# Gathering the rows of six heads for the first four tokens while the other two heads are picked

## The reference

```python
def block(xblk):
    q = (xblk @ w_q).astype(jnp.float32).reshape(PEER_BLOCK, PEER_HEADS, 2, PEER_DK // 2)
    s1 = jnp.einsum('thd,kd->thk', q[:, :, 0], k1)
    s2 = jnp.einsum('thd,kd->thk', q[:, :, 1], k2)
    t1, i1 = lax.top_k(s1, PEER_TOPK)
    t2, i2 = lax.top_k(s2, PEER_TOPK)
    ...
    top, pos = lax.top_k(cand, PEER_TOPK)
    eidx = jnp.take_along_axis(cidx, pos, axis=-1)
    gate = jax.nn.softmax(top, axis=-1).astype(xblk.dtype)
    u = expert_u[eidx]
    act = jax.nn.gelu(jnp.einsum('td,thkd->thk', xblk, u))
    v = expert_v[eidx]
    return jnp.einsum('thk,thkd->td', gate * act, v)
```

## Time and profile before

| | |
|---|---|
| median of 3 runs | 3699.09 us (3698.78 to 3702.22) |
| the profiled execution | 3699.25 us, its span 3697.4 us |
| PE busy | 3109.4 us (84%) |
| PE weight load busy | 2080.7 us (56%) |
| DVE busy | 1774.6 us (48%) |
| ACT busy | 613.5 us (17%) |
| POOL busy | 788.1 us (21%) |
| moved by DMA | 1096 MB, of which 671 MB by POOL's gathers |
| chain that ended last | PE 44%, DMA 28%, DVE 16%, issue 8% |

### The profile page before, as it was taken

How to read it: one execution, slowest core, us unless ns; L and a number is a source line. 1 busy time by engine, 2 the same in 40 slices (tenths; PEclk the granted TensorE clock), 3 DMA queues, 4 the chain that set the end, 5 groups by cost and what they waited for, 6 DMA issues and landing times.

```text
span 3697.4 us, 49910 instructions
## 1 busy us (share of the span) xinstructions
PE 3109.4 (84%) x17550; PEld 2080.7 (56%) x17550; DVE 1774.6 (48%) x4188; ACT 613.5 (17%) x1631; POOL 788.1 (21%) x891
## 2 busy tenths in 40 slices
PE   8998999999998999999999999888655666665564
PEld 7766777777776699998888887555300000000000
DVE  2397656665665200017333333468944444444444
ACT  1001222222222100001111111121211111111211
POOL 1000111211121000001222222233333333333332
PEclk9999999999999999999999999888755555555555
DMA  5434333333332688877999999999999999999997
GB/s 196 144 124 142 120 120 121 122 119 120 121 126 82 229 285 294 293 243 286 420 418 419 417 419 417 412 408 417 365 416 418 418 418 415 418 417 415 413 417 295
DMA packets 203478, 1096.05 MB, mean 296 GB/s; under 512 B 27360, under 2 KB 69216, under 8 KB 75952
## 3 DMA queue, kind: packets, MB, share of 16 engines
q0 software_dynamic: 92160, 671.13, 44.2%
q1 hardware_dynamic: 104096, 401.31, 30.2%
q10 hardware_dynamic: 7120, 22.22, 1.5%
HBM read 1062.88 MB, written 31.70 MB: 296 GB/s over the span
## 4 chain that ended last, share of the span: by engine, by line
PE 44%; DMA 28%; DVE 16%; issue 8%; POOL 2%; ACT 2%; DVEq 0%; SPq 0%; ACTq 0%; POOLq 0%
PE psum L519 27%; DMA branches<-in_peer_u,idx 22%; PE psum L605 7%; DMA ring<-in_peer_u,idx 4%; DVE branches L1431 2%; PE psum L974 2%; DVE branches L1929 2%; DVE branches L1534 2%; PE psum L684 1%; PE psum L675 1%; DVE ring L1929 1%; PE psum L681 1%; DVE rs L1642 1%; POOL ring L2017 1%; PE psum L349 1%
## 5 line engine op out<-in xcount | busy, mean ns | idle before, releaser
L1929 DVE CUSTOM_DVE_ANT_0 ring<-ring,psum 128x1024 f32<-128x1024 f32 x480 | 566.7, 1218 | 624.5 <-DMA ring<-in_peer_u,idx 575.7
L519 PE MATMUL psum<-hT,ring 128*128 128x128 f32 (+2 forms) x4800 | 801.6, 328 | 19.3 <-DMA ring<-in_w_glu 9.0
L519 PEld LDWEIGHTS psum<-hT,ring 128*128 128x128 f32 x4800 | 718.4, 195 | 94.5 <-issue 22.4
L957 PE MATMUL psum<-shared,selb 24*128 24x512 bf16 x1280 | 300.9, 520 | 451.8 <-DVE dots L1929 448.7
L957 PEld LDWEIGHTS psum<-shared,selb 24*128 24x128 bf16 x1280 | 56.1, 96 | 1017.1 <-DVE dots L1929 926.2
L605 PE MATMUL psum<-hT,ring 128*128 128x320 f32 x2112 | 621.6, 436 | 1.0 <-issue 1.0
L605 PEld LDWEIGHTS psum<-hT,ring 128*128 128x128 f32 x2112 | 381.8, 191 | 142.0 <-issue 18.4
L1291 ACT ACTIVATE ge<-dots 128x1 f32<-128x1 f32 x320 | 94.4, 295 | 1512.8 <-DVE dots L1929 1512.8
L1929 DVE CUSTOM_DVE_ANT_0 branches<-branches,psum 128x1024 f32<-128x1024 f32 x160 | 188.9, 1218 | 242.1 <-DMA branches<-in_peer_u,idx 228.7
L519 PE MATMUL psum<-branches,ring 128*128 128x128 f32 (+1 forms) x2048 | 296.1, 303 | 0.0
L519 PEld LDWEIGHTS psum<-branches,ring 128*128 128x128 f32 x2048 | 286.7, 193 | 3.4 <-issue 3.4
(11 more groups left out here) (403 smaller groups left out, 2864.5 us busy)
## 6 DMA issues: line engine op xcount, KB each, us to landing
ring<-in_w_merge SPq DMA_DIRECT2D x160, 1024.0 KB, 5.5
ring<-in_w_head SPq DMA_DIRECT2D x64, 1024.0 KB, 4.8
ring<-in_w_outp SPq DMA_DIRECT2D x32, 1024.0 KB, 7.0
ring<-in_w_pq SPq DMA_DIRECT2D x32, 1024.0 KB, 8.7
ring<-in_w_att SPq DMA_DIRECT2D x24, 1024.0 KB, 6.0
ring<-in_w_mem SPq DMA_DIRECT2D x16, 1024.0 KB, 4.8
ring<-in_w_glu SPq DMA_DIRECT2D x16, 1024.0 KB, 6.0
out_qkv_out<-ring ACTq DMA_DIRECT2D x16, 520.5 KB
```

The source lines that it names most:

```text
L519: last = mat(out, ring[:, j, (k0 + kt) * P:(k0 + kt + 1) * P], src[:, kt, :], start=kt == 0, stop=kt == kts - 1)
L957: last = mat(ps[q][:, :], selb[32 * q:32 * q + 24, j, :], hb[32 * q:32 * q + 24, g_, :], start=True, stop=True)
L1929: v.tensor_tensor_reduce(out=u, in0=u, in1=x, scale=1.0, scalar=0.0, op0=ALU.mult, op1=ALU.add, accum_out=dots[:, g_, j, half_:half_ + 1]) ...
```

## The change

The numbers of the first six heads are turned as soon as these heads are picked. For the first four tokens, POOL gathers the 96 rows of these heads at once, for `peer_u` in all four slots and for `peer_v` in three (the fourth is `vmem`). When all heads are picked, the last 32 numbers of each of the four tokens are copied separately (`idx_late`, since they must start at partition 0 for a gather of their own), and the 32 missing rows are gathered. Each semaphore of a slot counts 16 more from then on. `lists_ready` counts one more in all waits behind it.

TensorE does merge tiles 0, 1 and 2 after the turn of six heads, spreads the first token right behind the full lists, and turns the gates and does merge tiles 3 and 4 after that (`first_gates`). On DVE the copy of the gates moves behind `merge_cx(0)`, and `merge_d(0)` behind the first token's dots. The gates' turn goes to bank 4, and DVE zeroes the bank after its copy. POOL's first two groups of eight tokens are written out in Python instead of being the first turn of a hardware loop.

```diff
@@ -327,6 +327,9 @@
         in_memq, MEM_PARTS = (in_mem, w_in[4], w_in[5]), ((0, 4), (4, 10), (10, 16))
 
         SLOTS = 4
+        idx_late = sb("idx_late", [P, 4], U32)
+        FIRST_HEADS = 6
+        FIRST_ROWS = FIRST_HEADS * TOPK
         part_taken = sem("part_taken")
         summed = sem("summed")
         spread, w_ready, ge_ready, idx_ready, g8_ready = sem("spread"), sem("w_ready"), sem("ge_ready"), sem("idx_ready"), sem("g8_ready")
@@ -853,17 +856,22 @@
 
             for b in two:
                 pe.wait_ge(scores_read[b], PH)
-            for k in range(2):
+            pe.wait_ge(picked, FIRST_HEADS)
+            nc.tensor.transpose(ps[3][0:FIRST_ROWS, 0:P], tk0["efull"][:, 0, 0:FIRST_ROWS], ident[:]).then_inc(lists_turned, 1)
+            for k in range(3):
                 merge_tile(0, k)
             pe.wait_ge(picked, PH)
+            nc.tensor.transpose(ps[3][0:P - FIRST_ROWS, P:2 * P], tk0["efull"][:, 0, FIRST_ROWS:], ident[:])
+            nc.tensor.transpose(ps[0][:, 0:P], tk0["efull"][:, 0, :], ident[:]).then_inc(lists_turned, 1)
             nc.tensor.transpose(ps[2][:, 0:P], tk0["efull"][:, 0, :], ident[:]).then_inc(summed, SLOTS - 1)
-            nc.tensor.transpose(ps[0][:, 0:P], tk0["efull"][:, 0, :], ident[:]).then_inc(lists_turned, 1)
-            merge_tile(0, 2)
-            pe.wait_ge(picked, PH + 1)
-            nc.tensor.transpose(ps[1][:, 0:P], tk0["gfull"][:, 0, :], ident[:]).then_inc(lists_turned, 1)
-            nc.tensor.transpose(ps[2][:, P:2 * P], tk0["gfull"][:, 0, :], ident[:]).then_inc(summed, 1)
-            for k in range(3, 5):
-                merge_tile(0, k)
+
+            def first_gates():
+
+                pe.wait_ge(picked, PH + 1)
+                nc.tensor.transpose(ps[4][:, 0:P], tk0["gfull"][:, 0, :], ident[:]).then_inc(lists_turned, 1)
+                nc.tensor.transpose(ps[4][:, P:2 * P], tk0["gfull"][:, 0, :], ident[:]).then_inc(summed, 1)
+                for k in range(3, 5):
+                    merge_tile(0, k)
 
             def out_tile(m):
                 arrived("out1", m % 4, m // 4)
@@ -941,7 +949,7 @@
                         scores1((s - PQ_AT) // 2)
                 elif s in TURN_X2:
                     if TURN_X2[s] == 4:
-                        pe.wait_ge(lists_ready, 4)
+                        pe.wait_ge(lists_ready, 5)
                     turn_tokens(TURN_X2[s])
                 elif s == LISTS_AT:
                     turn_lists()
@@ -967,7 +975,7 @@
                     if beside:
                         second_block(16 * i + r)
                     pe.wait_ge(w_ready, 16 * i + r + 1)
-                    pe.wait_ge(v_in[s], 64 * i + 16 * (r // 4) + 16)
+                    pe.wait_ge(v_in[s], 64 * i + 16 * (r // 4) + 32)
                     if r % group == 0:
                         pe.wait_ge(acc_read[g_], i)
                     for q in range(4):
@@ -977,6 +985,7 @@
 
             pe.wait_ge(lists_ready, 2)
             spread_token(0, 0)
+            first_gates()
             for i in range(8):
                 pair(i, beside=True)
             with pe.Fori(8, PAIRS - 1) as i:
@@ -1317,10 +1326,10 @@
                         if beside:
                             second_block(16 * i + group * g_ + j)
 
-            act.wait_ge(lists_ready, 2)
+            act.wait_ge(lists_ready, 3)
             for i in range(8):
                 act_pair(i, first=i == 0, beside=True)
-            act.wait_ge(lists_ready, 4)
+            act.wait_ge(lists_ready, 5)
             for t, (start, end) in enumerate(SPANS):
                 with act.Fori(max(start, 8), end) as i:
                     act_pair(i)
@@ -1852,14 +1861,23 @@
             for h in range(PH):
                 for part in range(4):
                     topk_part(tk0, h, part)
+                    if h == FIRST_HEADS and part == 0:
+                        dve.wait_ge(lists_turned, 1)
+                        v.tensor_copy(eT[0:FIRST_ROWS, 0:N0], ps[3][0:FIRST_ROWS, 0:N0]).then_inc(lists_ready, 1)
             gates_in(tk0, 0)
             v.memset(ps[5], 0.0).then_inc(dotted[1], SLOTS)
-            dve.wait_ge(lists_turned, 1)
-            v.tensor_copy(eT[:, 0:N0], ps[0][:, 0:N0]).then_inc(lists_ready, 1)
+            dve.wait_ge(lists_turned, 2)
+            v.tensor_copy(idx_late[0:P - FIRST_ROWS, :], ps[3][0:P - FIRST_ROWS, P:P + 4])
+            v.tensor_copy(eT[FIRST_ROWS:, 0:N0], ps[0][FIRST_ROWS:, 0:N0]).then_inc(lists_ready, 1)
             gates_out(tk0, 0)
-            st(v.memset(ps[4], 0.0))
-            dve.wait_ge(lists_turned, 2)
-            v.tensor_copy(gT[:, 0:N0], ps[1][:, 0:N0]).then_inc(lists_ready, 1)
+
+            def first_gates():
+
+                dve.wait_ge(lists_turned, 3)
+                dve.wait_ge(summed, SLOTS)
+                v.tensor_copy(gT[:, 0:N0], ps[4][:, 0:N0]).then_inc(lists_ready, 1)
+                dve.wait_ge(lists_ready, 3)
+                v.memset(ps[4], 0.0)
 
             def merge_cx(i):
                 dve.wait_ge(merged_ready, KT + i)
@@ -1876,7 +1894,6 @@
 
             dve.wait_ge(parts_out, 16)
             merge_cx(0)
-            merge_d(0)
 
             def second_block(s):
 
@@ -1914,14 +1931,14 @@
                 elif s == LISTS_AT:
                     gates_out(tk1, 1)
                 elif s == LISTS_AT + 1:
-                    dve.wait_ge(lists_turned, 3)
+                    dve.wait_ge(lists_turned, 4)
                     v.tensor_copy(eT[:, N0:], ps[6][:, 0:N1]).then_inc(lists_ready, 1)
-                    dve.wait_ge(lists_turned, 4)
+                    dve.wait_ge(lists_turned, 5)
                     v.tensor_copy(gT[:, N0:], ps[7][:, 0:N1]).then_inc(lists_ready, 1)
 
             def dot(i, r):
                 s, g_, j = r % 4, r // group, r % group
-                dve.wait_ge(u_in[s], 64 * i + 16 * (r // 4) + 16)
+                dve.wait_ge(u_in[s], 64 * i + 16 * (r // 4) + 32)
                 for half_ in two:
                     dve.wait_ge(spread, 32 * i + 2 * r + half_ + 1 + 24)
                     u = u_slots[s][:, half_ * 1024:(half_ + 1) * 1024]
@@ -1929,9 +1946,12 @@
                     v.tensor_tensor_reduce(out=u, in0=u, in1=x, scale=1.0, scalar=0.0, op0=ALU.mult, op1=ALU.add,
                                            accum_out=dots[:, g_, j, half_:half_ + 1]).then_inc(dotted[half_], 1)
 
+            first_gates()
             for i in range(8):
                 for r in range(2 * group):
                     dot(i, r)
+                    if i + r == 0:
+                        merge_d(0)
                     second_block(16 * i + r)
             st(v.memset(r3[:], 1.0))
             for t, (start, end) in enumerate(SPANS):
@@ -2023,27 +2043,54 @@
                     pool.wait_ge(rest_ready, m)
                 g.tensor_tensor(hres0, hres0, parts[:, m, :], ALU.subtract).then_inc(rest_ready, 1)
 
+            def gather(table, slot, rows_, index, arrived_):
+                g.indirect_dma_start(slot[rows_, :], None, table, bass.IndirectOffsetOnAxis(ap=index, axis=0)).then_inc(arrived_, 16)
+
+            all_rows, early_rows, late_rows = slice(0, P), slice(0, FIRST_ROWS), slice(FIRST_ROWS, P)
+
+            def gather_token(n, g_, j, late=False):
+
+                s = j % 4
+                if not isinstance(n, int):
+                    pool.to_reg(n + 1)
+                pool.wait_ge(lists_ready, 2)
+                pool.wait_ge(dotted[1], n + 1)
+                every, some = idx8[:, g_, j:j + 1], idx_late[0:P - FIRST_ROWS, s:s + 1]
+                gather(io["peer_u"], u_slots[s], late_rows if late else all_rows, some if late else every, u_in[s])
+                pool.wait_ge(lists_ready, 2)
+                pool.wait_ge(summed, n + 1)
+                if late and s == 3:
+                    gather(io["peer_v"], v_slots[s], early_rows, idx8[early_rows, 0, j:j + 1], v_in[s])
+                gather(io["peer_v"], v_slots[s], late_rows if late else all_rows, some if late else every, v_in[s])
+
             def gather_pair(i):
                 for g_ in two:
                     g.tensor_copy(idx8[:, g_, :], eT[:, bass.ds(16 * i + 8 * g_, group)]).then_inc(idx_ready, 1)
-                    pool.wait_ge(idx_ready, 2 * i + g_ + 1)
+                    pool.wait_ge(idx_ready, 2 * i + g_ + 2)
                     for j in range(group):
-                        s, n = j % 4, 16 * i + group * g_ + j
-                        at_ = bass.IndirectOffsetOnAxis(ap=idx8[:, g_, j:j + 1], axis=0)
-
-                        pool.to_reg(n + 1)
-                        pool.wait_ge(lists_ready, 1)
-                        pool.wait_ge(dotted[1], n + 1)
-                        g.indirect_dma_start(u_slots[s], None, io["peer_u"], at_).then_inc(u_in[s], 16)
-                        pool.wait_ge(lists_ready, 1)
-                        pool.wait_ge(summed, n + 1)
-                        g.indirect_dma_start(v_slots[s], None, io["peer_v"], at_).then_inc(v_in[s], 16)
```

(21 more changed lines are left out.)

## The result

The change makes the kernel slower. Its median is 3713.15 us (3708.23 to 3718.21, 9 runs) against 3699.09 us (3697.1 to 3702.22, 9 runs): +14.1 us, ratio 1.0036 [1.0026, 1.0046]. The prediction was 3689.8 us. The profiled execution took 3716.04 us, its span 3714.2 us. I call this moment the scores' end, although the last four products with the keys come behind it, and line up the executions of all kernels by it. The early gathers are those of 96 rows (heads one to six), the late ones those of 32 (heads seven and eight). Tile (1,0) is the first merge tile of step 1, the first work of TensorE that needs token 0's dots.

What follows compares the result with a forecast made beforehand. It took TensorE to bound the first half and a full DMA path the second. TensorE 8.4 us earlier and the DMA path 9.7 us were taken as 9.5 us off: 3699.25 - 9.5 = 3689.8 us, range 3686.8 to 3695.5.

Steps and rivals of the forecast that it cites:

- Is the path full from then on?: From 1727.4: 8.4 MB of gathers and 6.3 MB of weights against 10.6 MB capacity, so the queue never runs dry.
- the sum: Whole kernel: TensorE 8.4 us earlier, DMA path 9.7 us; 9.5 us taken off the profiled execution.
- The weights beside them: Merge weight tiles of 1.05 MB, 6.3 MB until 1752.7, sharing a path counted at 0.42 MB per us with the gathers.
- The late rows: Token 0's last rows, queued behind 5.5 MB, land near 1748, at worst 1753.6; dots end at 1750.4, at worst 1756.
- rival C: Early rows and weights only change places, late rows arrive last, TensorE gains under 5 us: 3694.2 to 3699, chance 0.09.
- The prediction's own sign of being wrong: In the new profile, token 0's dots starting after 1750.5 would count against the forecast.
- TensorE: Tile (1,0) starts at 1753.1 instead of 1761.54: 5.4 us from idle stretch and low clock, 3.0 from waits behind tile 4.
- After 1968 the DMA decides: Late in the kernel, any TensorE gain above 0.6 us lets the DMA's 9.7 us through if the path stays full.
- The shift passes 2650: Around 2650 DVE's second picking decides, but DVE enters late or early with the DMA, so the shift passes through.
- Rival A: Gathers hold up picking of heads seven and eight by 6.6 us; put at 3694 us, chance 0.10.
- the port of POOL and DVE: Early gathers' effect on picking heads seven and eight costed at nothing; bounds 0 and 6.6 us.
- Rival D: POOL's issue of nine late gathers delays token 4's rows; at 4 us each 15.5 us lost, 3705 us, chance 0.04.

Runs made afterwards that it cites:

- experiment 5: The change with four heads gathered early, not six: rows on alternating even and odd partitions 3690.04 us; in blocks on partitions 0-63 and 64-127 3718.06 us.
- experiment 2: The change with its early gathers moved behind the wait for the full lists, the split kept: 3714.56 us, ratio 1.0038.
- experiment 1: The change with nothing gathered early and whole gathers of 128 rows, its new order kept: 3697.16 us against 3699.85, ratio 1.0004.

## Why the prediction was wrong

**The step that failed** is in "Is the path full from then on?" and the sum: "the new one moves 27.6 us x 0.42 = 11.6 MB". The path was full, but 0.42 MB per us was read from stretches in which every gather has 128 rows, and no row of before shows one with fewer. The gathers of 96 rows move 0.24 alone, and the path with them and the weights about 0.26. From 1725 to 1755 the kernel after moved 5 x (113+256+261+261+267+259) = 7.1 MB in place of the 11.6, and less than the 7.54 of before; over the 80 us it is (346 - 269) x 80 = 6.2 MB short. That is a resource which the trace of before doesn't show, and it had no bounds from both sides. With the alternating partitions, where the speed is kept, the same reasoning holds: 3690.0 us, from bytes moved while the heads are picked. That this is nearly the forecast of 3689.8 is partly luck, as that kernel gathers 64 rows early and not 96.

**The weights beside them** were taken to be as fast as ever. They are not. The DMA queues in 25 us of the kernel after (packets, MB, share of 16 engines):

```profile
q1 hardware_dynamic: 475, 3.40, 55.2%
q0 software_dynamic: 467, 3.06, 46.6%
```

and in 40 us of the full path before, from 1800 to 1840:

```profile
q0 software_dynamic: 1421, 10.36, 62.3%
q1 hardware_dynamic: 890, 6.37, 38.2%
```

A packet of weights (q1) takes 0.552 x 25 x 16 / 475 = 0.46 us of an engine against 0.382 x 40 x 16 / 890 = 0.27 before, and one of the gathers 0.40 against 0.28. The two kernels of experiment 5 show that the partitions of the gathers do this: in the 20 us from 8.2 us behind the scores' end a packet of weights takes 0.28 us beside the alternating gathers (574 packets, 50.0%) and 0.49 beside those in blocks (335 packets, 50.8%). That is why the early gathers gained nothing in experiment 2's comparison.

**The late rows.** "Near 1748", at worst 1753.6; they came at 1774.1. The mechanism of rival C was right in its first half (weights and early rows first, late rows last), but its price was again taken at 0.42: the 11 MB ahead of them at 0.262 MB per us take 42 us, and from 1728.7 (the first gather's start and 1.4 us) that is 1770.6. So the bound was a bound of the order, not of the speed. The prediction's own sign of being wrong, token 0's dots after 1750.5, is met: they start at 1774.13.

**TensorE.** Predicted 8.4 us earlier; 15.6 later in the change (13.7 by the scores' end), and 9.1 earlier by the scores' end with whole gathers (experiment 1). The tile arithmetic was right, the late rows were not. The first tile started 3.0 us behind the scores' end against 1.3 before, 1.7 us lost where 1.8 were predicted.

**"After 1968 the DMA decides"** was right and carries the table: 9 us of TensorE's time give 2.7 at most, and the bytes give theirs. In the kernel after too the gathers' landings of 30.32 and 31.28 us stand in the chain at 1993 and 2124, where before has 30.20 and, at 2108.04, 30.27. That is within the 1.3 us of the prediction. **The shift passes 2650** was right within some 2 us: the kernel after is 16.4 us late at the pair of 2010 (2026.66), 19.0 at that of 2175 (2193.79) and 16.8 at the last dots, where the medians differ by 14.1.

**Rival A and the port of POOL and DVE.** Costed at nothing, and right: no run here shows the gathers and DVE to hold each other up. Head six ends at 1724.52 and head eight at 1740.98 in the kernel after: 16.46 us with 0.28 of the new copy in it, against 16.30 for the same two heads before. The comparison of the earlier trace rows with early gathers beside it, the first line, is unchanged:

```profile
L1824 DVE TENSOR_TENSOR vmem<-vmem,iota x8: 691/693/694, 1679.3 to 1738.9; 128x512 bf16<-128x512 bf16 x8
```

**Rival D** (POOL's issue) was the only slower case and had the wrong mechanism: the pitch is 1.16 to 1.22 us. The case that came true, a path that is full and slow, was not in the list: all rivals took the speed of the path as given, and 0.05 for "slower" was far too little.

## What to carry to other kernels

Before a transfer is cut in two, ask on which partitions each piece lands: gathers on 96 and 32 neighbouring partitions left the path at six tenths of its speed, with the weights beside them slowed too, and so did a cut into 64 and 64 neighbouring ones, while a cut into the 64 even and the 64 odd partitions cost the path nothing. A DMA share of 1.0 says that the engines are busy, not that they are fast; read GB/s beside it, and count the bytes of a stretch whenever a later stage is bound by them. A speed read from one shape of transfer is no speed for another: where the trace shows none of the new shape, the range must have a case in which it is slower.

## What the runs showed of the hardware

- Gathers of 8 KB rows, alone on the chip, by destination partitions: 0-127 429 GB/s, 32-95 376, 0-111 291, 32-127 257, 0-95 239, 8-127 223, 0-119 222, 0-63 211, 64-127 208, all at a DMA share of 0.98 to 1.02.
- POOL's pitch hardly depends on the number of rows: 1.24 us for 128 rows, 1.21 for 96, 1.19 for 64, 1.16 for 32. Gathers of 32 rows can therefore not go much beyond 226 GB/s, wherever they land; the fullest 5 us showed 233.
- A gather of 127 rows is broken into small pieces: in 40 us of that group 10,752 of 11,326 packets were under 512 bytes, it moved 119 GB/s, and POOL's issue took 2.53 us in place of 0.94. Eight such gathers took 95 us (3718.61 to 3813.47), against 24 us for eight of 128 rows. With 124 rows it was 165 GB/s, 1.28 us per issue and 1,926 of 2,754 packets under 512 bytes.
- A slow destination slows other queues: the weights' packets, which go to all 128 partitions, took 0.46 us beside the gathers of the change and 0.49 beside those in blocks of 64, against 0.27 in before and 0.28 beside gathers on alternating partitions.
